# Linear layers of a hybrid encoder step: one matmul on unsplit 32-bit operands instead of three on rounded parts, weights in a ring of four pairs

## The chip, the cores and the metric

The kernel runs on one core of a Trainium2 chip. The metric is the device time of one execution in microseconds (us), as the median of several runs. The engines are named as in the profile: PE is TensorE's matmul side and PEld its weight load, DVE is VectorE, ACT ScalarE, POOL GpSimd, SP SyncE (here only an issuer of DMAs).

## The reference, cut to what matters

One inference step of two layers is computed for 512 prompt tokens and 32 sample tokens, which the kernel keeps side by side as 544 columns. Every sub-layer is a norm, a shift and scale from a condition vector, the sub-layer itself, a second norm, a gate and a residual addition. All inputs are float32.

```python
def swiglu(h, w_gate, w_up, w_down):
    return (jax.nn.silu(h @ w_gate) * (h @ w_up)) @ w_down

def forward(x, c, w, past):
    for l in range(DEPTH):                      # DEPTH = 2, D_MODEL = 1024, D_FF = 4096
        mod = (jax.nn.silu(c) @ w['ada_w'][l] + w['ada_b'][l]).reshape(B, 3, 3, D_MODEL)
        x = ffn_sublayer(x, w, mod, l, 0, 0)
        h = modulate(x, w['norm_pre'][l, 1], mod[:, 1, 0], mod[:, 1, 1])
        y, st = mixer_ab(...) if l % 2 == 0 else mixer_gdn(...)
        x = add_branch(x, y, w['norm_post'][l, 1], mod[:, 1, 2], 1.0)
        x = ffn_sublayer(x, w, mod, l, 2, 1)
```

The attention mixer (ab) has one input projection (`h @ ab_w_in`), two groups of eight heads and one output projection; the recurrent mixer (gdn) has one input projection, a short convolution, a chunked triangular solve with a scan over chunks, and one output projection. The linear layers are thus four feed-forwards of three matrices each and four projections.

## The kernel before, in words

**Units and pairs.** All weights of the linear layers are laid out in DRAM in the order of use, as 232 pairs of 1 MB (`w_stream`). A pair is two units; a unit makes one tile of 128 output features for all 544 tokens. Its weights are eight blocks of 128x128 (k = 0 to 7 over 1024 inputs), and the tokens are two halves of 272 columns (b), which go to two PSUM banks. Unit 0 of a pair uses banks 0 and 1, unit 1 banks 2 and 3. Each of the four feed-forwards has four blocks (kb) of 12 pairs: eight pairs of a gate tile and an up tile, then four pairs of the down projection. The attention input has 15 pairs, the recurrence's input 17, the two output projections 4 each.

**Three matmuls for one product.** Weights and activations are split into a high part, rounded to the type float32r, and a low part, the rest. A product of a block is `w_hi*hi + w_hi*lo + w_lo*hi`, three matmuls into the same bank (line 578; in a stage's first pair, line 600). So a unit has 48 matmuls and a pair 96.

**Who makes the parts.** GpSimd makes the weights' parts, per unit `w_hi` (line 491) and `w_lo` (line 494), from `raw`, two slots of one pair. There is one `w_hi` and one `w_lo` per unit of a pair, so GpSimd waits for `unit_done` of the pair before, and TensorE waits for `w_split` ahead of each unit. SP loads the next pair into a slot of `raw` once both units in it are split (line 477). VectorE and ScalarE make the activations' parts: after a norm, VectorE scales a row (line 1576), ScalarE applies shift and scale once or twice (line 1115), VectorE casts every other row (line 1581) and subtracts (line 1583). Within a feed-forward VectorE multiplies gate and up (line 1603), casts (line 1606) and subtracts (line 1608). Attention's outputs and the recurrence's gated outputs are cast and subtracted too.

**The order around it.** All engines run instruction lists written out by hand, with loops where a list repeats. `first_pair` is a stage's first pair: TensorE waits for one activation row k after the other (`h_ready`), and unit 1 follows unit 0 by four rows. In the first three feed-forwards VectorE also sums products for later modulation vectors, two instructions per gate and up pair (line 1532), and TensorE turns the sums with matmuls of one column, a quarter of them between the two units of each down pair (line 562, `ada_total`). Line 616 and line 609 sum squares over the features with a matrix of ones, in plain float32. In the attention's input stage TensorE computes score dots between units; in the recurrence's input stage it sums squared lengths between pairs (line 855), and near the end sums those of the sample (line 862). Between a stage's last matmul and the next stage's first come sums of squares (line 1593 on VectorE), a reciprocal root, the addition to x (VectorE six rows of eight, GpSimd two: `add_branch`) and a new norm. GpSimd splits the next stage's first pair before its additions.

The lines that the change touches most are `split_unit` and `split_pair` on GpSimd, `unit` and `first_pair` on TensorE, `modulate` on ScalarE, and `normalise` and `ffn` on VectorE.

Of the kernel before, what the change touches and what calls it, by code (L numbers as in the profile page):

```python
# [15 lines left out]
F32 = mybir.dt.float32  # L16
F32R = mybir.dt.float32r
# [4 lines left out]
P = 128  # L22
D = 1024
# [23 lines left out]
OUT_PAIRS = KD // 2  # L47
PAIRS = 4 * FFN_PAIRS + AB_PAIRS + GDN_PAIRS + 2 * OUT_PAIRS

# [13 lines left out]
def first_pairs():  # L63

    at, out = 0, {}
    for name, n in (("ffn0", FFN_PAIRS), ("ab_in", AB_PAIRS), ("ab_out", OUT_PAIRS), ("ffn1", FFN_PAIRS),
                    ("ffn2", FFN_PAIRS), ("gdn_in", GDN_PAIRS), ("gdn_out", OUT_PAIRS), ("ffn3", FFN_PAIRS)):
        out[name] = at
        at += n
    assert at == PAIRS and PAIRS % 2 == 0  # L70
    return out
# [46 lines left out]
def build(nc, io):  # L118
    with ExitStack() as ctx:
# [9 lines left out]
        hid_hi = sb("hid_hi", [P, KD, T], F32R)  # L129
        hid_lo = sb("hid_lo", [P, KD, T], F32R)  # L130
        h_at = nc.sbuf_base
        h_hi = sb("h_hi", [P, KD, T], F32R)
        h_lo = sb("h_lo", [P, KD, T], F32R)
        raw = sb("raw", [P, 2, 2, D])
        w_hi = sb("w_hi", [P, 2, D], F32R)
        w_lo = sb("w_lo", [P, 2, D], F32R)
# [31 lines left out]
        h32 = cut("k t", k=2, t=T)  # L168
# [76 lines left out]
        g_sq, g_out = cut("r t", r=2, t=T), cut("r t", r=2, t=T)  # L245
# [14 lines left out]
        w_loaded = [sem("w_loaded0"), sem("w_loaded1")]  # L260
        w_rounded = sem("w_rounded")
        w_split = sem("w_split")
# [21 lines left out]
        h32_ready = sem("h32_ready")  # L284
        h_rounded = sem("h_rounded")
        h_ready = sem("h_ready")
        hid_rounded = sem("hid_rounded")
        hid_ready = sem("hid_ready")
# [28 lines left out]
        o_rounded = sem("o_rounded")  # L317
# [59 lines left out]
        g_own = sem("g_own")  # L377
# [81 lines left out]
        def _(sp):  # L459
# [11 lines left out]
            for s in range(2):  # L471
                sp.dma_start(raw[:, s], io["w_stream"][s]).then_inc(w_loaded[s], 16)
            with sp.Fori(1, PAIRS // 2) as i:
                for s in range(2):
# [12 lines left out]
        def _(pool):  # L487
            pool.wait_ge(consts, 1)
# [8 lines left out]
            def split_pair(i, s):  # L497

                for u in range(2):
                    pool.wait_ge(w_loaded[s], 16 * i + 16)  # L500

                    pool.wait_ge(unit_done, 4 * i + 2 * s + u - 1)
                    split_unit(s, u, 4 * i + 2 * s + u)

            def split_pairs(a, b):
                if a % 2:
                    split_pair(a // 2, 1)
                with pool.Fori(a // 2 + a % 2, b // 2) as i:
                    for s in range(2):
                        split_pair(i, s)  # L510
                if b % 2:
                    split_pair(b // 2, 0)

# [9 lines left out]
            pool.wait_ge(w_loaded[0], 16)  # L523
            for u in range(2):
                split_unit(0, u, u)

            done = 1
            ends = [FIRST[name] + 1 for name in ("ab_in", "ffn1", "ffn2", "gdn_in", "ffn3")] + [PAIRS]
# [7 lines left out]
        def _(pe):  # L536
# [30 lines left out]
            def unit(u, n, hi, lo, ready=None, tail_ready=None):  # L567

                pe.wait_ge(w_split, 2 * n + u + 1)
                pe.wait_ge(bank_free[u], n + 1)  # L570
                for k in range(KD):
                    if ready:
                        ready(k)
                    for b in range(2):
                        w = slice(k * P, (k + 1) * P)
                        t = slice(b * HT, (b + 1) * HT)
                        for i, (a, m) in enumerate(((w_hi, hi), (w_hi, lo), (w_lo, hi))):
                            mm = pe.matmul(psum[:, 2 * u + b, 0:HT], a[:, u, w], m[:, k, t],  # L578
                                           start=(k == 0 and i == 0), stop=(k == KD - 1 and i == 2))
                mm.then_inc(unit_done, 1)  # L580

            def first_pair(n, hi, lo, ready):


                for u in range(2):
                    pe.wait_ge(bank_free[u], n + 1)
                pe.wait_ge(w_split, 2 * n + 2)
                lag = KD // 2
                for step in range(KD + lag):
                    for u in range(2):  # L590
# [5 lines left out]
                        for b in range(2):  # L596
                            w = slice(k * P, (k + 1) * P)
                            t = slice(b * HT, (b + 1) * HT)
                            for i, (a, m) in enumerate(((w_hi, hi), (w_hi, lo), (w_lo, hi))):
                                mm = pe.matmul(psum[:, 2 * u + b, 0:HT], a[:, u, w], m[:, k, t],  # L600
# [1615 lines left out]
```

## Time and profile before

The median of three runs is 3967.1 us (3966.59 to 3969.22). The profiled execution's own span is 3966.7 us; the page gives no time around it.

| engine | busy us | share of the span | instructions |
|---|---|---|---|
| PE | 3697.3 | 93% | 26506 |
| PEld | 3441.6 | 87% | 26506 |
| DVE | 1991.0 | 50% | 2200 |
| ACT | 580.2 | 15% | 1157 |
| POOL | 2197.0 | 55% | 956 |

Matmuls are pipelined, and one's duration covers its whole way through the array; a matmul's rate is therefore read from the starts of a series, not from the duration of one. The granted clock of TensorE is 1.00 (2.4 GHz) in most slices of the span; it falls to 0.53 in one slice of the recurrence. 343 MB move by DMA, 86 GB/s over the span. The stages in order of time: modulation head to about 70 us, first feed-forward to 724, attention input to 976, attention to 1228, its output projection to 1280, second feed-forward to 1959, third to 2593, recurrence's input to 2866, solve and recurrence to 3271, its output projection to 3321, fourth feed-forward to 3939, last addition and store to the end.

### The profile page before, as it was taken

To read this page: it belongs to the slowest core of one execution; us is meant where nothing else is said; L and a number is where in the kernel's file an instruction comes from. 1 tells how busy PE (TensorE), PEld (TensorE's weight loads), DVE (VectorE), ACT (ScalarE), POOL (GpSimd) and SP (SyncE) were. 2 spreads that over 40 slices of the span, in tenths; PEclk is the share of its full clock that TensorE was granted. 3 is DMA by queue.
4 is the path that set the end of the run, shared out by engine and by line. 5 is a ranking of instruction groups with operands and counts; after the bars stand their busy time and mean duration, and the time that the engine had idled before them with its cause. 6 is when DMAs were issued, how large, how long until landed. Compare 5 with 4: busy or idle time off the path is not lost.

```text
span 3966.7 us, 63424 instructions
## 1 busy us (share of the span) xinstructions
PE 3697.3 (93%) x26506; PEld 3441.6 (87%) x26506; DVE 1991.0 (50%) x2200; ACT 580.2 (15%) x1157; POOL 2197.0 (55%) x956
## 2 busy tenths in 40 slices
PE   6999999899999899999899999989889997999997
PEld 3999999778567899999789999978878777999997
DVE  5734636549533737356553443566765335322334
ACT  2000000321332200000210000042132123000001
POOL 3767767556003567667666777756600005777775
PEclk9999999899789999999899999989999658999998
DMA  5333323243001324223122232212300001222221
GB/s 204 136 108 111 136 101 118 78 107 131 7 22 43 106 97 144 106 106 140 64 95 101 105 113 100 101 56 75 79 9 1 1 1 54 85 87 93 85 85 65
DMA packets 80752, 342.75 MB, mean 86 GB/s; under 512 B 13960, under 2 KB 17544, under 8 KB 50936
## 3 DMA queue, kind: packets, MB, share of 16 engines
q1 hardware_dynamic: 36976, 248.02, 17.6%
q10 hardware_dynamic: 43656, 93.04, 7.3%
q8 instruction: 86, 1.41, 0.1%
q14 instruction: 34, 0.28, 0.0%
HBM read 329.93 MB, written 11.11 MB: 86 GB/s over the span
## 4 chain that ended last, share of the span: by engine, by line
PE 74%; issue 12%; POOL 6%; DVE 5%; ACT 2%; ACTq 1%; POOLq 0%; DVEq 0%
PE psum L578 61%; POOL w_lo L494 3%; POOL w_hi L491 2%; PE psum L562 2%; DVE arena L1532 1%; PE psum L1001 1%; PE psum L983 1%; PE psum L943 1%; PE psum L955 1%; PE psum L1004 1%; PE psum L1002 1%; PE psum L958 1%; ACTq L1141 1%; PE psum L545 1%; PE psum L616 1%
## 5 line engine op out<-in xcount | busy, mean ns | idle before, releaser
L491 POOL TENSOR_TENSOR w_hi<-raw,one_col 128x1024 fp32r<-128x1024 f32 x464 | 934.7, 2014 | 1682.9 <-PE psum L600 829.4
L578 PE MATMUL psum<-h_hi,w_hi 128*128 128x272 f32 x5120 | 1489.5, 291 | 21.9 <-POOL w_lo L494 16.1
L578 PE MATMUL psum<-h_hi,w_lo 128*128 128x272 f32 x5120 | 1481.5, 289 | 0.0
L578 PE MATMUL psum<-h_lo,w_hi 128*128 128x272 f32 x5120 | 1477.8, 289 | 0.0
L494 POOL TENSOR_TENSOR w_lo<-raw,w_hi 128x1024 fp32r<-128x1024 f32 x464 | 1221.2, 2632 | 36.4
L578 PEld LDWEIGHTS psum<-h_hi,w_hi 128*128 128x128 f32 x5120 | 965.2, 189 | 43.1 <-issue 42.0
L578 PEld LDWEIGHTS psum<-h_lo,w_hi 128*128 128x128 f32 x5120 | 965.4, 189 | 0.2 <-issue 0.2
L578 PEld LDWEIGHTS psum<-h_hi,w_lo 128*128 128x128 f32 x5120 | 964.5, 188 | 0.0
L578 PE MATMUL psum<-hid_hi,w_hi 128*128 128x272 f32 x2048 | 607.4, 297 | 0.6
L578 PE MATMUL psum<-hid_hi,w_lo 128*128 128x272 f32 x2048 | 600.1, 293 | 0.0
L578 PE MATMUL psum<-hid_lo,w_hi 128*128 128x272 f32 x2048 | 598.0, 292 | 0.0
L1603 DVE TENSOR_TENSOR arena<-arena,psum 128x544 f32<-128x544 f32 x128 | 92.3, 721 | 655.8 <-PE psum L578 635.9
L1615 DVE TENSOR_TENSOR arena<-arena,psum 128x544 f32<-128x544 f32 x128 | 92.1, 720 | 643.9 <-PE psum L578 643.9
L578 PEld LDWEIGHTS psum<-hid_hi,w_hi 128*128 128x128 f32 x2048 | 394.5, 193 | 3.4 <-issue 1.9
L578 PEld LDWEIGHTS psum<-hid_lo,w_hi 128*128 128x128 f32 x2048 | 394.5, 193 | 0.0
L578 PEld LDWEIGHTS psum<-hid_hi,w_lo 128*128 128x128 f32 x2048 | 393.4, 192 | 0.0
L1135 ACT ACTIVATE arena<-psum 128x544 f32<-128x544 f32 x128 | 80.0, 625 | 2096.2 <-PE psum L578 2092.0
L1532 DVE SCALAR_TENSOR_TENSOR arena<-arena,c_t 128x1536 f32<-128x1536 f32 (+1 forms) x182 | 368.3, 2064 | 0.0
L1608 DVE TENSOR_TENSOR hid_lo<-arena,hid_hi 128x544 fp32r<-128x544 f32 x128 | 358.4, 2800 | 4.4
L1606 DVE CAST hid_hi<-arena 128x544 fp32r<-128x544 f32 x128 | 193.3, 1510 | 4.4
L600 PE MATMUL psum<-h_hi,w_hi 128*128 128x272 f32 x256 | 84.1, 329 | 40.7 <-DVE h_lo L1583 39.2
L562 PEld LDWEIGHTS psum<-ones,arena 128*128 128x128 f32 x528 | 72.3, 214 | 38.5 <-DVE arena L1532 37.6
(284 smaller groups left out, 3328.3 us busy)
## 6 DMA issues: line engine op xcount, KB each, us to landing
raw<-in_w_stream SPq DMA_DIRECT2D x232, 1024.0 KB, 4.8
arena<-in_ada_w ACTq DMA_DIRECT2D x72, 768.0 KB, 5.6
arena<-in_ada_w ACTq DMA_DIRECT2D x32, 384.0 KB, 4.3
spare<-in_ada_w ACTq DMA_DIRECT2D x5, 768.0 KB, 16.9
rel_spread<-arena ACTq DMA_DIRECT2D x1, 3072.0 KB
spare_h<-in_ada_w ACTq DMA_DIRECT2D x3, 768.0 KB, 15.7
x<-in_x_t SPq DMA_DIRECT2D x1, 2176.0 KB, 18.6
out_y_t<-x SPq DMA_DIRECT2D x1, 2176.0 KB, 7.0
```

What stands on the lines that cost most here:

```text
L491: pool.tensor_tensor(w_hi[:, u], raw[:, s, u], one_col[:].broadcast_to([P, D]), ALU.mult)\
L494: pool.tensor_tensor(w_lo[:, u], raw[:, s, u], w_hi[:, u].bitcast(F32), ALU.subtract)\
L545: mm = pe.matmul(psum[0:2, b, :], c_t[:, k, :], ada_second[k][:, b * 512:(b + 1) * 512], start=(k == 0), stop=(k == KD - 1))
L562: mm = pe.matmul(psum[:, 7, 2 * t + g:2 * t + g + 1], ada_sum[:, g, t * P:(t + 1) * P], ones[:, 0:1], start=True, stop=True)
L578: mm = pe.matmul(psum[:, 2 * u + b, 0:HT], a[:, u, w], m[:, k, t], start=(k == 0 and i == 0), stop=(k == KD - 1 and i == 2))
L600: mm = pe.matmul(psum[:, 2 * u + b, 0:HT], a[:, u, w], m[:, k, t], start=(k == 0 and i == 0), stop=(k == KD - 1 and i == 2))
L1135: act.activation(split(silu[:, j % 2]), halves(0), ACT.Silu).then_inc(bank_free[0], 1)
L1532: op = dve.scalar_tensor_tensor(ada_sum[:, g, 0:n], ada_w[:, k, 0:n], c_t[:, k, g:g + 1], ada_sum[:, g, 0:n], ALU.mult, ALU.add)
L1603: dve.tensor_tensor(split(h32[:, j % 2]), split(silu[:, j % 2]), halves(2), ALU.mult)\
L1606: dve.tensor_copy(hid_hi[:, j], h32[:, j % 2]).then_inc(hid_rounded, 1)
L1608: dve.tensor_tensor(hid_lo[:, j], h32[:, j % 2], hid_hi[:, j].bitcast(F32), ALU.subtract)\
L1615: dve.tensor_tensor(split(y[:, m]), split(y[:, m]), halves(2 * (m % 2)), ALU.add)\
```

## The change

The type float32r, the parts and everything that makes them go. `w_ring` holds four pairs of unsplit weights, and the activations are one float32 tile each, `h_in` after a norm and `hid` within a feed-forward (the room that the parts had stays allocated, since other stages reuse it). A product is one matmul instruction in the program, on two float32 operands. SP loads a slot of the ring as soon as `unit_done` says that TensorE has done both units of the pair that was in it; TensorE waits for a pair's load itself, once per pair (`pair_loaded`). GpSimd keeps only its share of `add_branch`. On ScalarE a row takes one pass after a norm, whose end is `h_ready`; on VectorE the casts and subtractions go, and a down projection's rows are ready when `bank_free[1]` counts the multiplication of gate and up. Because a wait for a load has to name a slot, TensorE's lists are written out over a block of 12 pairs (first block apart, then a loop over three), where they were loops over single pairs.

```diff
-            with sp.Fori(1, PAIRS // 2) as i:
-                for s in range(2):
-                    sp.wait_ge(w_split, 4 * i - 2 + 2 * s)
-                    sp.dma_start(raw[:, s], io["w_stream"][2 * i + s]).then_inc(w_loaded[s], 16)
+            with sp.Fori(1, PAIRS // SLOTS) as i:
+                for s in range(SLOTS):
+                    sp.wait_ge(unit_done, 2 * (SLOTS * (i - 1) + s + 1))
+                    sp.dma_start(w_ring[:, s], io["w_stream"][SLOTS * i + s]).then_inc(w_loaded[s], 16)
...
-            def split_unit(s, u, n):
-                pool.tensor_tensor(w_hi[:, u], raw[:, s, u], one_col[:].broadcast_to([P, D]), ALU.mult)\
-                    .then_inc(w_rounded, 1)
-                pool.wait_ge(w_rounded, n + 1)
-                pool.tensor_tensor(w_lo[:, u], raw[:, s, u], w_hi[:, u].bitcast(F32), ALU.subtract)\
-                    .then_inc(w_split, 1)
...
-            for n, end in enumerate(ends):
-                split_pairs(done, end)
-                done = end
+            for n in range(LAYERS * SUBS):
                 add_branch(n)
...
-            def unit(u, n, hi, lo, ready=None, tail_ready=None):
-                pe.wait_ge(w_split, 2 * n + u + 1)
+            def unit(u, n, slot, of, ready=None):
                 pe.wait_ge(bank_free[u], n + 1)
                 for k in range(KD):
                     if ready:
                         ready(k)
                     for b in range(2):
-                        w = slice(k * P, (k + 1) * P)
-                        t = slice(b * HT, (b + 1) * HT)
-                        for i, (a, m) in enumerate(((w_hi, hi), (w_hi, lo), (w_lo, hi))):
-                            mm = pe.matmul(psum[:, 2 * u + b, 0:HT], a[:, u, w], m[:, k, t],
-                                           start=(k == 0 and i == 0), stop=(k == KD - 1 and i == 2))
+                        mm = pe.matmul(psum[:, 2 * u + b, 0:HT], w_ring[:, slot, u, k * P:(k + 1) * P],
+                                       of[:, k, b * HT:(b + 1) * HT], start=(k == 0), stop=(k == KD - 1))
                 mm.then_inc(unit_done, 1)
+            def pair_loaded(at, rounds=0):
+                pe.wait_ge(w_loaded[at % SLOTS], 16 * (at // SLOTS + 1 + rounds))
...
-                    for to in (h32[:, k % 2], h_hi[:, k])[:2 - k % 2]:
-                        for g, (a, b) in enumerate(GROUPS):
-                            op = act.activation(to[:, a:b], tmp[:, k % 2, a:b], ACT.Identity,
...
-                    op.then_inc(h32_ready, 1)
+                    for g, (a, b) in enumerate(GROUPS):
+                        op = act.activation(h_in[:, k, a:b], tmp[:, k % 2, a:b], ACT.Identity,
...
+                    op.then_inc(h_ready, 1)
...
-                        dve.tensor_tensor(split(h32[:, j % 2]), split(silu[:, j % 2]), halves(2), ALU.mult)\
+                        dve.tensor_tensor(split(hid[:, j]), split(silu[:, j % 2]), halves(2), ALU.mult)\
                             .then_inc(bank_free[1], 1)
-                        dve.wait_ge(bank_free[1], n + 2)
-                        dve.tensor_copy(hid_hi[:, j], h32[:, j % 2]).then_inc(hid_rounded, 1)
-                        dve.wait_ge(hid_rounded, q + j + 1)
-                        dve.tensor_tensor(hid_lo[:, j], h32[:, j % 2], hid_hi[:, j].bitcast(F32), ALU.subtract)\
-                            .then_inc(hid_ready, 1)
```

## Rows read from the trace of the kernel before

**Rows 1.** The page: busy us of an engine, share of the span, instructions.
```profile
PE 3697.3 (93%) x26506; PEld 3441.6 (87%) x26506; DVE 1991.0 (50%) x2200; ACT 580.2 (15%) x1157; POOL 2197.0 (55%) x956
```

**Rows 2.** The page: the chain that ended last, by line, shares of the span.
```profile
PE psum L578 61%; POOL w_lo L494 3%; POOL w_hi L491 2%; PE psum L562 2%; DVE arena L1532 1%; PE psum L1001 1%; PE psum L983 1%; PE psum L943 1%; PE psum L955 1%; PE psum L1004 1%; PE psum L1002 1%; PE psum L958 1%; ACTq L1141 1%; PE psum L545 1%; PE psum L616 1%
```

**Rows 3.** The chain in order of time (start, us, what, count): last feed-forward.
```profile
3369.28 570.06 PE psum L578 x4512
```

**Rows 4.** Single lines: count, duration in ns as min/median/max, first and last start.
```profile
L616 PE MATMUL psum<-arena,ones x192: 392/393/822, 42.0 to 3345.8; 128*128 128x272 f32 x192
...
L904 PE MATMUL psum<-arena x136: 275/275/554, 2884.6 to 3086.4; 128*128 128x128 f32 x136
...
L545 PE MATMUL psum<-spare,c_t x30: 591/592/1057, 28.9 to 53.2; 128*2 128x512 f32 x30
```

**Rows 5.** TensorE in order of time: start, us from first start to last end, count.
```profile
2934.95 1.06 PE L904 MATMUL psum<-arena 128*128 128x128 f32 x8
...
53.65 7.89 PE L545 MATMUL psum<-spare_h,c_t 128*2 128x512 f32 x18
```

**Rows 6.** Windows, one per stage: length, busy us (count) of each engine, PEclk, DMA.
```profile
91.30:723.70 632.40, 610.67 (x4704) 604.73 (x4704) 344.81 (x200) 32.79 (x53) 455.24 (x189) 0.98 0.32 116
...
771.10:976.10 205.00, 197.89 (x1450) 181.50 (x1449) 121.15 (x210) 38.16 (x70) 124.57 (x57) 0.98 0.38 103
...
2006.90:2592.90 586.00, 581.85 (x4608) 580.17 (x4608) 249.85 (x200) 32.82 (x53) 427.73 (x189) 1.00 0.29 105
...
2640.80:2853.00 212.20, 203.31 (x1497) 192.97 (x1497) 156.20 (x140) 51.30 (x105) 142.00 (x61) 0.98 0.22 75
...
3368.40:3939.30 570.90, 570.06 (x4513) 569.21 (x4512) 192.51 (x133) 32.78 (x53) 403.33 (x187) 1.00 0.23 83
```

**Rows 7.** The same window view, for line 562 alone: PE and PEld busy us (count).
```profile
2006.90:2592.90 586.00, 12.02 (x96) 12.16 (x96) 1.00 0.29 105
```

**Rows 8.** TensorE in order of time, with the idle us before and its releaser.
```profile
189.89 1.44 PE L562 MATMUL psum<-ones,arena 128*128 128x1 f32 x6 [4.08 <-DVE arena L1532]
```

**Rows 9.** VectorE in order of time: the end of a gate and up block.
```profile
171.96 5.18 DVE L1532 SCALAR_TENSOR_TENSOR arena<-arena,c_t 128x1536 f32<-128x1536 f32 x2
...
173.69 3.45 DVE L1532 SCALAR_TENSOR_TENSOR arena<-arena,c_t 128x1536 f32<-128x1536 f32 x1
...
179.68 0.72 DVE L1603 TENSOR_TENSOR arena<-arena,psum 128x544 f32<-128x544 f32 x1 [2.55 <-PE psum L578]
```

**Rows 10.** The chain of waits: end of the recurrence's input.
```profile
2780.79 1.72 PE psum L855 x4
...
2835.07 5.64 PE psum L862 x32
...
2854.21 0.41 ACT arena L1369
...
2884.61 2.05 PE psum L904 x8
```

**Rows 11.** The chain of waits: the norm before the last feed-forward.
```profile
3347.74 0.74 DVE arena L1576
...
3352.06 1.12 ACT arena L1115 x2
```

**Rows 12.** TensorE in order of time: the last feed-forward's first matmul.
```profile
3351.53 0.57 PE L600 MATMUL psum<-h_hi,w_hi 128*128 128x272 f32 x1 [5.32 <-DVE h_lo L1583]
```

**Rows 13.** Windows around that first pair: the seventh column is the granted clock.
```profile
3354.00:3356.00 2.00, 1.92 (x11) 1.59 (x9) 1.75 (x4) 1.58 (x4) 0.00 (x0) 0.64 0.00 0
```

**Rows 14.** Line 1593: count, duration in ns as min/median/max.
```profile
L1593 DVE TENSOR_TENSOR arena<-arena x42: 718/1944/2645, 690.1 to 3942.1; 128x544 f32<-128x544 f32 x42
```

**Rows 15.** Waits of SP's queue: us in total, times, longest us.
```profile
SPq L477 <- POOL w_lo L494: 3720.4, 230, 417.4
```

**Rows 16.** DMA issues: count, KB each, median us to landing.
```profile
raw<-in_w_stream SPq DMA_DIRECT2D x232, 1024.0 KB, 4.8
```

**Rows 17.** Waits of the weight load: us in total, times, longest us.
```profile
PEld psum L578 <- issue: 44.1, 72, 1.7
```

More of the change, by code:

```diff
@@ L259, in build @@
         out_stored = sem("out_stored")
-        w_loaded = [sem("w_loaded0"), sem("w_loaded1")]
-        w_rounded = sem("w_rounded")
-        w_split = sem("w_split")
+        w_loaded = [sem(f"w_loaded{s}") for s in range(SLOTS)]
         unit_done = sem("unit_done")
@@ L596, in first_pair @@
                         for b in range(2):
[L597 to L600, printed above, removed]
-                                               start=(k == 0 and i == 0), stop=(k == KD - 1 and i == 2))
+                            mm = pe.matmul(psum[:, 2 * u + b, 0:HT], w_ring[:, n % SLOTS, u, k * P:(k + 1) * P],
+                                           of[:, k, b * HT:(b + 1) * HT], start=(k == 0), stop=(k == KD - 1))
                         if k == KD - 1:
@@ L644, in ffn, with pair @@
-                first_pair(n0, h_hi, h_lo, lambda k: pe.wait_ge(h_ready, KD * n_pre + k + 1))
-                with pe.Fori(1, KD) as j:
-                    gate_up(n0 + j)
-                downs(0, n0)
+                per = FFN_PAIRS // KB
+                def pair(at, kb, of, ready=None, between=None):
+                    slot = at % SLOTS
+                    pair_loaded(at, per // SLOTS * kb)
+                    unit(0, at + per * kb, slot, of, ready)
+                    if between:
+                        between()
+                    unit(1, at + per * kb, slot, of)
@@ new lines, in downs, with total @@
+                def downs(kb):
+                    def ready(k):
+                        pe.wait_ge(bank_free[1], n0 + per * kb + k + 2)
+                    for j in range(KD // 2):
+                        total = None
+                        if ADA_PARTS[f]:
+                            def total():
+                                ada_total(ADA_CHUNKS_BEFORE[f] + kb, ADA_PARTS[f], j)
+                        pair(n0 + KD + j, kb, hid, None if j else ready, total)
+                first_pair(n0, h_in, lambda k: pe.wait_ge(h_ready, KD * n_pre + k + 1))
@@ L648, in ffn @@
+                for j in range(1, KD):
+                    pair(n0 + j, 0, h_in)
+                downs(0)
                 with pe.Fori(1, KB) as kb:
-                    first = n0 + kb * (FFN_PAIRS // KB)
-                    with pe.Fori(0, KD) as j:
-                        gate_up(first + j)
-                    downs(kb, first)
+                    for j in range(KD):
+                        pair(n0 + j, kb, h_in)
+                    downs(kb)
             pe.wait_ge(c_ready, 1)
@@ L662, in _, with pair_of, product @@
             norm_sum(2)
-            def product(first, pairs, hi, lo, ready=None):
+            def pair_of(n, of):
+                pair_loaded(n)
+                for u in range(2):
+                    unit(u, n, n % SLOTS, of)
+            def product(first, pairs, ready=None):
                 if ready:
-                    first_pair(first, hi, lo, ready)
-                with pe.Fori(first + bool(ready), first + pairs) as n:
-                    unit(0, n, hi, lo)
-                    unit(1, n, hi, lo)
+                    first_pair(first, h_in, ready)
+                for n in range(first + bool(ready), first + pairs):
+                    pair_of(n, h_in)
             def rel_bias():
@@ L1733, in outputs @@
             def outputs(e):
-                mixer, i, h = items[e]
+                mixer, i, head = items[e]
                 k0 = 4 * (mixer == "B")
```

134 lines of the change are left out of this document (36 added, 98 removed).

## The prediction

> **What bounds the kernel now.** I read the page's busy times first: TensorE has work in flight for 93% of the span [rows 1]. The chain of work that ended last comes next: 61% of the span is line 578 alone, the matmuls of the linear layers, and the two splitting lines of GpSimd (491 and 494) follow with 5% together [rows 2]. So TensorE's rate is the bound, and GpSimd enters only where TensorE waits for a split. The chain of the last feed-forward stage has no such wait: 4512 matmuls in 570.06 us without a break, 126.3 ns from one start to the next [rows 3]. Three of them make one product of a 128x128 weight block with 272 tokens: 379 ns. A pair of units has 32 such products: 12.13 us, and there are 232 pairs.
>
> **The price of one unsplit product.** The trace already holds plain 32-bit matmuls. Each that the kernel issues stands as two instructions: the six row sums of line 616 issue 96, and the trace has 192 [rows 4]. What one costs from start to start at 272 columns I take from both sides. Eight of 128 columns with a new stationary block each run in 1.06 us, less the last one's 0.275, over 7: 112 ns; eighteen of 512 columns in 7.89 us, less 0.592, over 17: 429 ns [rows 4, 5]. The durations are 275, 393 and 592 ns for 128, 272 and 512 columns [rows 4], so 272 columns are 118 above the first and 199 below the second: 112 + 118 = 230 and 429 - 199 = 230. I take 230 ns, with 228 and 234 as ends (the durations leave the rate of a long dense stream open). One product is then 2 x 230 = 460 ns against 379 for the three of today: two slow instructions cost more than three quick ones. A pair takes 64 x 0.230 = 14.72 us, 2.59 more than now; over 232 pairs that is +601.
>
> **What comes off, stage by stage** (stretches begin behind a stage's first pair) [rows 6].
> - Last feed-forward: 47 pairs x 14.72 = 691.8 for 570.9: +120.9.
> - Third: the same 47 pairs and the 96 small modulation matmuls of line 562, 12.0 us [rows 7], are 703.8 for 586.0: +117.8.
> - First and second: twice the small matmuls, 24, make 715.8 for 632.4: +83.4 each (the second has the same pattern). They take 632.4 - 598.0 = 34.4 more than the third with twice its small matmuls, and that is what the splits cost there today. Four times in each, TensorE stands 4.08 us before line 562 [rows 8], because VectorE has still to finish line 1532, behind the rounding and subtracting of the hidden tile. One of the two instructions of line 1532 takes 5.18 - 3.45 = 1.73 us and the other 3.45 while GpSimd reads beside it [rows 9]. Afterwards VectorE has 0.72 + 2 x 1.73 = 4.2 us behind the last gate and up pair, and TensorE fills 7.36 us with the first unit of the down projection before it asks: this wait goes, and nothing is late next. Were VectorE still to take 3.45 twice, 0.72 + 6.9 would be 0.3 over. If all of the 34.4 stayed in both stages, it is +69.
> - Attention's input: 14 pairs; the 35.2 us that today are not matmuls of line 578 (205.0 - 14 x 12.13: score dots and their waits for ScalarE) stay: +36.3.
> - Recurrence's input: 15 pairs 220.8, the row sums 8 x 1.72 and 5.6 [rows 10] are 240.2 for 212.2: +28.0. The stalls that vanish are VectorE's convolutions, which run beside GpSimd today. The sixteenth pair costs nothing: from ScalarE's line 1369 at 2854.21, which needs the fifteenth, a chain of 30.4 us leads to TensorE's next work at 2884.61 [rows 10], and 14.72 lies inside it.
> - The two output projections: 8 x 2.59 = +20.7.
> - First pairs, six after a normalisation: today VectorE's scaled row at 3347.74 leads, over two passes of ScalarE and a subtraction, to the first matmul at 3351.53 [rows 11, 12]. With one pass of 1.12 behind the 0.74 it is due at 3349.6: -1.9 each, -11.4. ScalarE then delivers a row in about 1.1 us and TensorE needs 0.92 or, at the clock granted there until about 3355 (half, 1.2 GHz) [rows 13], 1.84: it is TensorE that paces, and the pair takes some 14.7 and 2 for the clock, about the 16.9 of today. No gain there.
> - Stage ends: the last sum of squares (line 1593), for which TensorE waits, takes up to 2.65 beside GpSimd's split of the next stage's first pair, and 0.72 with GpSimd still [rows 14]: -1.9 at five ends, -9.5.
> - Attention itself, the solve and the recurrence hold no split; the outputs of attention lose one VectorE pass, worth 0 to -10; I take 0.
>
> Sum: 120.9 + 117.8 + 166.8 + 36.3 + 28.0 + 20.7 - 11.4 - 9.5 = +470 on the profiled execution's 3966.7, which is 0.4 below the median of the runs: 4436.
>
> **The ring and the queues.** SP's queue stood 3720 us for GpSimd's splits [rows 15]; now it stands for units of TensorE, four pairs back. A pair's megabyte lands in a median of 4.8 us [rows 16], and three pairs, 44 us, lie between a slot's release and its next use: TensorE's new wait for a load, once per pair, ends at once. Queued behind it is all that follows on TensorE, its pair first. By the same figures two slots would do: the ring gains nothing. At the start four megabytes are issued instead of two behind the same load; TensorE asks for the first only behind the head's modulation products. GpSimd loses 928 instructions and keeps its additions to x, now without splits queued ahead.
> TensorE's loops become longer and fewer: a turn holds twelve pairs. Waits put down to issue ahead of line 578's weight loads were 44.1 us in 72 times, 1.7 at most [rows 17], nearly all with matmuls still running. Twelve turns of 1.7 are 20, the upper bound; I take 0.
> The Trainium skill (Runtime: NRT & Kernel Launch, Instruction fetch mechanics) says that a taken branch to code outside the pages at hand stalls for a fetch; this trace has only short loops, and no row here shows what a long one costs.
>
> **Rivals.**
> 1. Each pass keeps the price of a pass in the dense stream. 272 columns in 126.3 ns are slower than the plain matmuls per column and pass (115 of 230), so the dense stream may carry something, 11 ns a pass, that short bursts do not show. Then a product is 4 x 126.3 = 505 ns, 45 above mine: 7424 x 0.0454 = +337, 4773. For it: the bursts of rows 5 last a microsecond or eight. Against it: line 855's four instructions of 512 columns, directly behind the dense matmuls, take 1.72 us, 430 each [rows 10], as slow as without that stream. By the Trainium skill (FP8 and Floating Point Precision, TensorE Precision Notes) a true 32-bit product is four passes through the array; counted in today's passes that is this rival, and the two instructions of double length here agree with the four. 7%.
> 2. Not slower: the two instructions of a product overlap, because they use the same weight block and tokens. It decides where an instruction's pace falls from 230 to 230 - 470/14.848 = 198 ns; if only one of the two counted, it would be 7424 x 0.230 less, near 2730. Against it: the pairs of rows 5 do not overlap. 3%.
> 3. A new wait takes the split's place: the turns of the longer loops, or late weights. A microsecond at each pair would be +232, 4668. For it: code and ring are new. Against it: rows 16 and 17. 5% beyond my range.
> 4. The ring frees nothing: that is my forecast already, and changes no number.
>
> **How the numbers follow.** My case has 85%. Its own range: 228 ns is -30 and attention -10, which makes 4396; 234 is +59, the splits' cost in the first two feed-forwards +69: 4505 at most of one alone. The range 4395 to 4520 leaves out the two slow rivals and the fast one, 15%. A measurement here tells 0.2%, 8 us, from no change. Faster 0.03, same 0.01, slower 0.96.
>
> **What would show it.** In the profile after: line by line, two instructions of 128x272 per product, 14848 in all, 229 to 232 ns from start to start in the last feed-forward's chain, some 692 us; no 4 us gap ahead of line 562's matmuls; SP waiting for TensorE; VectorE's last sum of squares at 0.72 at every stage end. A pace of 253 is rival 1; gaps once in twelve pairs are rival 3. I am wrong if the last feed-forward's stretch is below 660 or above 720.

## The result: slower by 11.3%, and the profile after

The kernel after takes 4413.8 us (median of four runs, 4406.4 to 4419.8) against 3967.4 (3966.6 to 3969.2): ratio 1.1126, interval 1.1110 to 1.1141. The forecast was 4436, 22 us above it. The profiled execution has a span of 4412.8, 446.1 more than before.

The page after: busy times [rows 1], then the chain that ended last by engine and by line [rows 2].

```profile
PE 4231.3 (96%) x19082; PEld 3414.2 (77%) x19082; DVE 1111.7 (25%) x1822; ACT 553.6 (13%) x1109; POOL 42.4 (1%) x28
...
PE 66%; DVE 2%; ACT 1%; issue 0%; ACTq 0%; DVEq 0%
PE psum L530 54%; PE psum L553 2%; PE psum L959 1%; PE psum L941 1%; PE psum L901 1%; PE psum L913 1%; PE psum L962 1%; PE psum L569 1%; PE psum L960 1%; PE psum L916 1%; PE psum L518 1%; DVE x L1583 0%; PE psum L862 0%; DVE arena L1581 0%; PE psum L928 0%
```

GpSimd is gone from the chain, which could be followed back to 1318.6 us only (its shares add up to 70% of the span, so they are not to be set beside those of rows 2). VectorE has lost 879 us of work, and TensorE has 7424 instructions fewer and yet more to do. The chain in order of time, as in rows 3 (line 530 is the old 578, line 518 the old 562, line 553 the first pair):

```profile
1544.46 1.23 PE psum L518 x12
1545.70 14.78 PE psum L530 x64
...
3696.05 689.35 PE psum L530 x3008
```

The last line gives the pace: 689.35 / 3008 = 229.2 ns from start to start, two of them 458 ns where three took 379. The small modulation matmuls follow the unit ahead of them without a gap; the 4.08 us of rows 8 are no longer there. The stages as windows, in the order and with the columns of rows 6:

```profile
90.03:800.80 710.77, 710.77 (x3200) 592.57 (x3199) 153.51 (x136) 32.73 (x53) 0.00 (x0) 1.00 0.32 103
844.43:1082.97 238.54, 232.39 (x1001) 179.60 (x1000) 94.59 (x222) 38.15 (x69) 0.00 (x0) 0.99 0.33 87
2189.13:2889.18 700.05, 700.05 (x3105) 581.90 (x3103) 105.50 (x136) 32.75 (x53) 0.00 (x0) 1.00 0.27 88
2933.11:3176.00 242.89, 238.62 (x1024) 191.13 (x1024) 79.44 (x140) 50.86 (x105) 0.00 (x0) 1.00 0.19 65
3696.05:4385.39 689.34, 689.34 (x3009) 571.17 (x3007) 48.98 (x69) 32.73 (x53) 0.00 (x0) 1.00 0.20 67
```

In the three feed-forward windows TensorE's busy time is the whole length: no gap is left, neither at a turn of the longer loops nor at a load. (The windows of the recurrence's input end at different work before and after; the table below goes to the stage's last matmul in both.)

Where the 446 us came from, by the first and last matmuls of each stage in the two traces (us, after less before; "ahead" is from the last matmul of the stage before to the first of this one, "rest" from behind the first pair to the last matmul):

```
stage               ahead   first pair   rest                forecast of the rest
first feed-forward   -1.9      +0.7      +78.3               +83.4
attention input      -4.4      +0.6      +33.6               +36.3
attention output     -7.0   3.6 + 6.6 = 10.2, whole stage    +10.4 (ahead: 0)
second feed-forward  -4.2      +1.1      +79.1               +83.4
third feed-forward   -4.6      +0.8     +114.0              +117.8
recurrence input     -4.9      +0.9      +32.4               +28.0
recurrence output    -0.1   2.4 + 6.6 = 9.0, whole stage     +10.4
last feed-forward    -4.3      -1.7     +118.4              +120.9
```

The rounded entries sum to +446. As a balance: 232 pairs at 14.67 instead of 12.13 us are +589, and 143 come back: 81 in the first two feed-forwards, 31 ahead of the stages, 13 in the first pairs, 17 in the rest (each rounded).

### The profile page after: what moved, and what is told of

It is laid out like the page before. It is cut to its first block, busy times and chain, and to the rows that moved or that the text cites. A ratio compares the mean times of both kernels' runs of the same rounds, so it can differ in the third digit from the quotient of the medians.

```text
span 4412.8 us, 44833 instructions
## 1 busy us (share of the span) xinstructions
PE 4231.3 (96%) x19082; PEld 3414.2 (77%) x19082; DVE 1111.7 (25%) x1822; ACT 553.6 (13%) x1109; POOL 42.4 (1%) x28
## 4 chain that ended last, share of the span: by engine, by line
PE 66%; DVE 2%; ACT 1%; issue 0%; ACTq 0%; DVEq 0%
PE psum L530 54%; PE psum L553 2%; PE psum L959 1%; PE psum L941 1%; PE psum L901 1%; PE psum L913 1%; PE psum L962 1%; PE psum L569 1%; PE psum L960 1%; PE psum L916 1%; PE psum L518 1%; DVE x L1583 0%; PE psum L862 0%; DVE arena L1581 0%; PE psum L928 0%
## 5 line engine op out<-in xcount | busy, mean ns | idle before, releaser
L530 PE MATMUL psum<-h_in,w_ring 128*128 128x272 f32 x10240 | 2356.6, 393 | 4.3 <-ACT spare L1308 4.3
L530 PEld LDWEIGHTS psum<-h_in,w_ring 128*128 128x128 f32 x10240 | 1945.1, 190 | 415.1 <-issue 14.9
L530 PE MATMUL psum<-hid,w_ring 128*128 128x272 f32 x4096 | 953.1, 393 | 0.0
L530 PEld LDWEIGHTS psum<-hid,w_ring 128*128 128x128 f32 x4096 | 774.6, 190 | 156.7
L1547 DVE TENSOR_TENSOR hid<-arena,psum 128x544 f32<-128x544 f32 x128 | 92.3, 721 | 1545.6 <-PE psum L530 1499.4
L1554 DVE TENSOR_TENSOR arena<-arena,psum 128x544 f32<-128x544 f32 x128 | 92.3, 721 | 849.6 <-PE psum L530 849.6
L1486 DVE SCALAR_TENSOR_TENSOR arena<-arena,c_t 128x1536 f32<-128x1536 f32 (+1 forms) x182 | 276.9, 1566 | 0.0
L553 PE MATMUL psum<-h_in,w_ring 128*128 128x272 f32 x512 | 136.0, 432 | 21.2 <-ACT h_in L1069 20.7
L553 PEld LDWEIGHTS psum<-h_in,w_ring 128*128 128x128 f32 x512 | 107.5, 212 | 48.9 <-issue 23.3
L569 PE MATMUL psum<-arena,ones 128*128 128x272 f32 x192 | 66.0, 509 | 31.4 <-ACT arena L1026 31.4
L518 PE MATMUL psum<-ones,arena 128*128 128x1 f32 x528 | 63.8, 246 | 0.0
L688 PE MATMUL psum<-arena 64*128 64x128 f32 (+3 forms) x128 | 59.4, 550 | 0.0
L901 PEld LDWEIGHTS psum<-spare_h 128*128 128x128 f32 x336 | 42.5, 196 | 14.7 <-DVE spare_h L1892 11.4
## 6 DMA issues: line engine op xcount, KB each, us to landing
x<-in_x_t SPq DMA_DIRECT2D x1, 2176.0 KB, 18.4
```

Source lines behind the costliest of these rows:

```text
L518: mm = pe.matmul(psum[:, 7, 2 * t + g:2 * t + g + 1], ada_sum[:, g, t * P:(t + 1) * P], ones[:, 0:1], start=True, stop=True)
L530: mm = pe.matmul(psum[:, 2 * u + b, 0:HT], w_ring[:, slot, u, k * P:(k + 1) * P], of[:, k, b * HT:(b + 1) * HT], start=(k == 0), stop=(k = ...
L553: mm = pe.matmul(psum[:, 2 * u + b, 0:HT], w_ring[:, n % SLOTS, u, k * P:(k + 1) * P], of[:, k, b * HT:(b + 1) * HT], start=(k == 0), stop ...
L569: mm = pe.matmul(psum[:, 4 + b, 0:HT], ones[:], sq[:, k % 2, b * HT:(b + 1) * HT], start=(k == 0), stop=(k == KD - 1))
L688: pe.matmul(psum[:, b, 0:n], z[r:r + HD, zq + c, i * P:(i + 1) * P], z[r:r + HD, zk + c, 0:n], start=True, stop=False, skip_group_check=(m ...
L901: mm = pe.matmul(psum[:, b + 3, t], low_m[:, u, t], inv_t[:, u, t], start=True, stop=True)
```

## Experiments

Ratios are to the kernel before on the same chip (3967.0 us for the first four, 3968.5 for the others).

**1. The ring with two slots.** The kernel after with one number changed:

```diff
-SLOTS = 4
+SLOTS = 2
```

> The changed kernel with a ring of two pairs instead of four. My theory: the ring adds nothing, because a pair's megabyte lands in 4.8 us and one pair of TensorE takes 14.67, so even with one pair between release and next use no load is late: 4414 us, within 8, and no gap of TensorE behind a wait for a load. Rival (the four slots hide loads that run into the 768 KB modulation loads): some of the 232 pairs wait a few us, 4450 or more, with TensorE's idle time put down to DMAs in the three feed-forwards that load modulation weights.

Measured: 4413.6 us (4409.6 to 4415.8), ratio 1.1125 [1.1107, 1.1144], and the stages as with four (the profiled executions differ in two stretches that hold no wait for a load: 4.6 us less in the recurrence, 2.7 more in the last first pair). The first feed-forward's window and SP's wait:

```profile
90.00:800.80 710.80, 710.75 (x3200) 593.19 (x3199) 153.56 (x137) 32.72 (x53) 0.00 (x0) 1.00 0.31 103
```

```profile
SPq L467 <- PE psum L530: 3205.2, 222, 21.4
```

710.80 with two slots, 710.77 with four. With four, SP's wait and the loads are these:

```profile
SPq L467 <- PE psum L530: 3193.3, 220, 21.4
```

```profile
w_ring<-in_w_stream SPq DMA_DIRECT2D x232, 1024.0 KB, 4.8
```

A load lands in 4.8 us where even two slots leave it a pair's 14.7. Two slots more are neither cost nor gain; what follows is about the arithmetic and about the work that went with the parts.

**2. GpSimd as busy as before, with nobody waiting for it.** The kernel of experiment 1; GpSimd rounds and subtracts on tiles of its own at the times of the old splits, and no matmul reads the results. It is added work only; the outputs come from the same arithmetic as in experiment 1.

```diff
+            def split_unit(n):
+                pool.tensor_tensor(w_hi[:], src[:], one_col[:].broadcast_to([P, D]), ALU.mult).then_inc(w_rounded, 1)
+                pool.wait_ge(w_rounded, n + 1)
+                pool.tensor_tensor(w_lo[:], src[:], w_hi[:].bitcast(F32), ALU.subtract).then_inc(w_split, 1)
...
+                split_pairs(done, end)
+                done = end
                 add_branch(n)
```

> The changed kernel with two slots, in which GpSimd again does the arithmetic of the old split, at its old places, but from a tile of its own into tiles that nobody reads; nobody waits for it except its own additions to x. It shows what the old kernel paid for GpSimd reading beside VectorE, without the casts, the subtractions and the waits for splits. My theory: only the stage ends come back (1.9 at five ends) and at most 0.3 at each of eight modulation sums, since 0.72 + 2 x 3.45 = 7.6 us on VectorE stand against 7.36 of TensorE: 4420 to 4435. Rival: the contention itself was what the first two feed-forwards paid, and their 34 us each come back: 4480.

Measured: 4432.5 us (4429.7 to 4438.1), ratio 1.1176 [1.1158, 1.1195]: 19 more than experiment 1. The time ahead of five stages grows by 2.3 to 3.1 us each, and ahead of attention's output by nothing (245.7 us, as in the kernel after). The rest of the 19 is made of smaller parts: 3.8 in the first two feed-forwards, 1.9 in attention's input, 4.4 in the recurrence (where experiment 1 had 4.6 less than the kernel after) and -4.7 in the first pairs. Line 1574 here is the last sum of squares of rows 14; first this kernel, then the kernel after (count, ns as min/median/max, first and last start):

```profile
L1574 DVE TENSOR_TENSOR arena<-arena x42: 718/1943/2645, 762.6 to 4406.1; 128x544 f32<-128x544 f32 x42
```

```profile
L1538 DVE TENSOR_TENSOR arena<-arena x42: 715/717/726, 760.8 to 4388.2; 128x544 f32<-128x544 f32 x42
```

With GpSimd busy it has the 718/1944/2645 of rows 14 to within a nanosecond, with GpSimd idle never more than 726. So the gain at the stage ends is GpSimd's silence, as the prediction said, at 2.3 to 3.1 us instead of 1.9; and what attention gained (-7.0) is not. The first two feed-forwards each pay 2 us and no more: the slow VectorE lines are back, but the rounding and subtracting ahead of them are not, and VectorE is done about when TensorE ends the first unit of the down projection, as the prediction reckoned.

GpSimd's own instruction, same kernel (busy us, mean ns):

```profile
L497 POOL TENSOR_TENSOR w_lo<-src,w_hi 128x1024 fp32r<-128x1024 f32 x464 | 1207.0, 2601 | 36.5
```

The longest addition to VectorE's 0.72 is 1.93 us, less than one such instruction of 2.6. What it depends on stands at the end of the stage before the last feed-forward, VectorE's two sums first, then GpSimd's two instructions:

```profile
3667.86 1.94 DVE L1574 TENSOR_TENSOR arena<-arena 128x544 f32<-128x544 f32 x1
...
3669.94 2.65 DVE L1574 TENSOR_TENSOR arena<-arena 128x544 f32<-128x544 f32 x1
```

```profile
3667.32 1.89 POOL L495 TENSOR_TENSOR w_hi<-src,one_col 128x1024 fp32r<-128x1024 f32 x1 [2.72 <-PE psum L566]
...
3669.30 2.71 POOL L497 TENSOR_TENSOR w_lo<-src,w_hi 128x1024 fp32r<-128x1024 f32 x1
```

Each sum ends just behind the GpSimd instruction that ran when it began: 3669.80 behind 3669.21, 3672.59 behind 3672.01, 0.59 and 0.58 us. So do 39 of the 42 of line 1574 in this trace and 39 of the 42 of line 1593 in the kernel before, each 0.58 to 0.59 us behind; the other three of each begin with GpSimd idle and take 0.72. A sum waits for the rest of the GpSimd instruction and only then runs. The Trainium skill (SBUF — State Buffer, Who interferes with whom) has it that a VectorE instruction with two inputs in SBUF contends with a GpSimd instruction that reads SBUF, and that the ports they share are an exclusive lock; the trace agrees, by these ends.

**3. The kernel before, with the small matmuls moved behind the second unit.** The split arithmetic stays.

```diff
                             unit(0, first + KD + j, hid_hi, hid_lo, None if j else ready)
-                            ada_total(ADA_CHUNKS_BEFORE[f] + kb, ADA_PARTS[f], j)
                             unit(1, first + KD + j, hid_hi, hid_lo)
+                            ada_total(ADA_CHUNKS_BEFORE[f] + kb, ADA_PARTS[f], j)
```

> The kernel before with one change: a quarter of the modulation sums (line 562) goes behind the second unit of a down pair instead of between its two units. My theory: TensorE then asks about 6 us later than today, VectorE is done, and the eight waits of 4.1 us and the slow clock behind each (about 2.2 us) go: some 50 us, 3917. Rival 1: the wait is only moved, since VectorE's next work or the rounding is late by as much: 3960 or more. Rival 2: the waits go but the clock loss has another cause: about 33 us, 3934.

Measured: 3903.7 us (3902.4 to 3910.7), ratio 0.9846 [0.9830, 0.9863]: 63 less than before. The first feed-forward's window (632.40 in rows 6):

```profile
91.30:692.10 600.80, 595.31 (x4695) 590.45 (x4695) 344.88 (x200) 32.81 (x53) 455.22 (x189) 1.00 0.34 122
```

The first two stages lose 31.4 and 30.5 of the 34.4 that the prediction had put down to the splits, the third 5.1. So 31 of those 34.4 go by the order of two lines, with all splits kept. They were the price of the splits' work on VectorE in that order only; the changed kernel removes them by taking the work away, and the kernel before can have them for nothing. VectorE's and GpSimd's busy times are those of rows 6, so it is the place of the wait and not the work that went. Half of the gain is the wait itself (TensorE is idle for 5.5 us of the window instead of 21.7), the other half is the clock behind it: busy time falls from 610.67 to 595.31 us, at a mean granted clock of 0.98 and 1.00. Behind the wait of rows 8 the trace has 0.50 (1.2 GHz) until some 197 us.

**4. The kernel before, with 16-bit parts.** Both rounded parts are bfloat16, still three matmuls; the parts carry fewer digits, so this computes less exactly than before.

```diff
-F32R = mybir.dt.float32r
+F32R = mybir.dt.bfloat16
...
```

> The kernel before with all high and low parts in bfloat16 instead of float32r: still three matmuls for a product, less exact. It asks why a pass of the old kernel takes 126 ns where 272 columns at 2.4 GHz are 113 and a plain 32-bit half takes 229 = 227 + 2. Theory A (the four-byte operands of the quick form cost about 10 ns a matmul): the pace falls to 116 ns, 22272 x 0.010 = 220 us off, 3745, less what GpSimd then bounds, since its 5.8 us a unit stand against 5.6 of TensorE in the first two feed-forwards. Theory B (a matmul with a new weight block each time cannot go quicker, whatever its type): 126 ns stays, and the time is within 30 us of 3967, lower only by quicker casts.

Measured: 3764.9 us (3762.9 to 3766.7), ratio 0.9489 [0.9473, 0.9505]. From its chain, a dense stretch of the last feed-forward:

```profile
3564.85 128.76 PE psum L580 x1110
```

128.76 / 1110 = 116.0 ns for the same 272 columns that took 126.3 [rows 3]. The page's lines of the high parts, matmuls and weight loads:

```profile
L580 PE MATMUL psum<-h_hi,w_hi 128*128 128x272 bf16 x5120 | 1431.5, 280 | 41.6 <-POOL w_lo L496 30.7
L580 PEld LDWEIGHTS psum<-h_hi,w_hi 128*128 128x128 bf16 x5120 | 501.4, 98 | 157.8 <-issue 65.1
```

A weight load is recorded at 98 ns here, at 189 for the parts of the kernel before and 190 for the 32-bit words of the kernel after. The 10 ns a pass therefore belonged to the four-byte quick form and not to dense streams. Whether the weight load or the moving operand carries it stays open: operands of mixed width were not tried.

**5. The kernel after, with the squared lengths one by one.** In the recurrence's input one row of squared lengths (line 814) stands behind each unit instead of two behind each pair.

```diff
-                    pair_of(n0 + p, h_in)
-
-                    for m in (2 * p - 6, 2 * p - 5):
+                    pair_loaded(n0 + p)
+                    for u in range(2):
+                        unit(u, n0 + p, (n0 + p) % SLOTS, h_in)
+                        m = 2 * p - 6 + u
                         if 0 <= m < 2 * NH:
```

> The changed kernel with one edit in the recurrence's input: the two squared lengths that stood behind a pair stand one behind each unit. It asks for the 0.61 us that TensorE still waits ahead of seven pairs there, which the prediction had taken for VectorE beside GpSimd. My theory now: a ring of waits (TensorE's lengths release ScalarE's squares, behind which stands ScalarE's copy of the next unit, behind which TensorE waits for the bank); with one length at a time the copy is done while the unit runs: the seven gaps fall below 0.3, some 4 us less, 4408 to 4412. Rival: ScalarE's copies follow VectorE's convolutions, and the gaps stay at 0.6 in their sum.

What it is to explain, from the kernel after: the chain between two pairs, and TensorE's next matmul with the idle time before it.

```profile
2994.34 0.87 PE psum L814 x2
...
2995.30 0.04 ACT arena L1318
...
2995.83 0.28 ACT arena L1307
...
2996.34 0.20 ACT spare L1308
...
2996.67 14.91 PE psum L530 x64
```

```profile
2996.67 0.70 PE L530 MATMUL psum<-h_in,w_ring 128*128 128x272 f32 x2 [0.61 <-ACT spare L1308]
```

Seven times TensorE stands 0.61 us for ScalarE's copies (lines 1307 and 1308), which free the accumulators, and ScalarE stands for TensorE's second squared length through its squares (1318). One run, not repeated: 4401.6 us, and TensorE between the same units:

```profile
2975.24 1.02 PE L814 MATMUL psum<-arena 128*128 128x512 f32 x2
2976.10 7.49 PE L530 MATMUL psum<-h_in,w_ring 128*128 128x272 f32 x32
2983.43 1.02 PE L814 MATMUL psum<-arena 128*128 128x512 f32 x2
2984.29 7.49 PE L530 MATMUL psum<-h_in,w_ring 128*128 128x272 f32 x32
```

Each group starts before the modelled end of the one ahead and none has an idle time; the seven gaps are gone, and the stage's rest is 6.0 us shorter. The gaps are 7 x 0.61 = 4.3 of it, and what TensorE loses in starting again is the rest: a pair with its two lengths takes 17.23 us in the kernel after and 2 x 8.19 = 16.38 here. The profiled execution is another 7 us shorter, and these are not the edit's: 4.4 lie ahead of the recurrence's output, where experiment 1, without this edit, has 4.6 less too, and the rest mostly in first pairs, which follow the clock (see below).

**6. Experiments 3 and 4 together.**

```diff
-F32R = mybir.dt.float32r
+F32R = mybir.dt.bfloat16
...
-                            ada_total(ADA_CHUNKS_BEFORE[f] + kb, ADA_PARTS[f], j)
                             unit(1, first + KD + j, hid_hi, hid_lo)
+                            ada_total(ADA_CHUNKS_BEFORE[f] + kb, ADA_PARTS[f], j)
```

> The kernel before with both edits: bfloat16 parts and the modulation sums behind the second unit. If the two gains are of different origin they add: 3765 - 63 = 3702. If with the quicker passes TensorE asks again before VectorE is done (a unit is now 5.6 us instead of 6.05), part of the waits stays: 3715 to 3735.

Measured: 3694.0 us (3691.5 to 3696.2), ratio 0.9310 [0.9294, 0.9325]; the sum of the two gains would have been 3702 (5.8 of the difference lie in attention, 259.9 us for the 265.7 of experiment 4). The window of the first feed-forward and what TensorE waits for:

```profile
91.19:652.03 560.84, 545.73 (x4696) 458.73 (x4695) 346.49 (x200) 32.74 (x53) 434.28 (x189) 1.00 0.36 131
```

```profile
PE psum L580 <- POOL w_lo L496: 35.4, 56, 1.0
```

The kernel before has this for the same wait:

```profile
PE psum L578 <- POOL w_lo L494: 16.1, 32, 0.9
```

560.84 - 545.73 = 15 us of this stage are idle. With quicker passes GpSimd's splits show more: 35.4 us over the whole kernel for 16.1.

**7. The same, with the hidden tile's rounding on ScalarE.**

```diff
                         act.activation(split(silu[:, j % 2]), halves(0), ACT.Silu).then_inc(bank_free[0], 1)
+                        act.wait_ge(bank_free[1], n + 2)
+                        act.activation(hid_hi[:, j], h32[:, j % 2], ACT.Copy).then_inc(hid_rounded, 1)
...
-                        dve.tensor_copy(hid_hi[:, j], h32[:, j % 2]).then_inc(hid_rounded, 1)
```

> As the kernel with bfloat16 parts and later sums, and ScalarE rounds the hidden tile's high part instead of VectorE. Theory: VectorE loses 1.5 us a gate and up pair, so it reads less beside GpSimd, GpSimd's splits end earlier, and the gaps of about 0.5 us ahead of TensorE's gate and up pairs in the first two feed-forwards shrink: some 20 us less, 3680. Rival: those gaps come from line 1532 alone, and nothing moves: 3702, or ScalarE's rounding delays its gate activations and it is slower.

Measured: 3677.8 us (3676.5 to 3678.8), ratio 0.9268 [0.9252, 0.9283], the fastest of all and ahead of both kernels. The same two views:

```profile
90.75:643.91 553.16, 545.73 (x4695) 458.73 (x4695) 301.96 (x168) 53.76 (x85) 434.82 (x189) 1.00 0.39 133
```

```profile
PE psum L580 <- POOL w_lo L496: 19.6, 44, 1.0
```

VectorE's 44 us of rounding went to ScalarE, which takes 21 us for it and had room, and the idle time of the stage halves from 15.1 to 7.4.

**8. The same, with GpSimd splitting the next stage's first pair behind its additions to x.**

```diff
-            ends = [FIRST[name] + 1 for name in ("ab_in", "ffn1", "ffn2", "gdn_in", "ffn3")] + [PAIRS]
+            ends = [FIRST[name] for name in ("ab_in", "ffn1", "ffn2", "gdn_in", "ffn3")] + [PAIRS]
```

> As the one with ScalarE's rounding, and GpSimd splits a stage's first pair behind its additions to x instead of ahead of them. Theory: the last sum of squares of a stage is then at 0.72 instead of up to 2.65, which is worth 1.9 at each of five stage ends: 9 us less than the kernel without this edit. Rival: the splits then run beside VectorE's additions to x, which are on the way to the next norm, and take back as much or more.

Measured: 3697.5 us (3696.6 to 3706.0), ratio 0.9324 [0.9308, 0.9339]: 20 slower than experiment 7. The chain at the stage end before the last feed-forward, first here, then in experiment 7:

```profile
3095.55 0.74 DVE arena L1597
...
3107.83 2.30 DVE x L1647
3110.13 2.58 DVE arena L1645
```

```profile
3079.59 2.43 DVE arena L1597
...
3086.47 1.73 DVE x L1647
3088.20 1.78 DVE arena L1645
```

The sum of squares is quick, as wanted, and the additions to x behind it pay instead, several of them. The contention moved to a place where it costs more; the first matmul behind each of the five stage ends is 3.3 to 5.2 us later than in experiment 7.

## Why the prediction was right, and where it missed

**The price held.** 230 ns a half product was taken from bursts of 128 and 512 columns [rows 4, 5]; 3008 in a row give 229.2. At 14848 instructions 0.8 ns is 12 us of the 22.

**Rival 1 (505 ns a product) fell** with that pace; 253 would have been its sign. Experiment 4 shows why: the 126 ns of the old passes held 10 ns that bfloat16 passes don't have, so they were no measure of what a plain pass costs. Its four passes stand, at a lower price: two recorded instructions of 229.2 are four times 114.6, near the 116.0 of a bfloat16 pass. The Trainium skill (FP8 and Floating Point Precision, TensorE Precision Notes) counts four passes for a true 32-bit product; in time the trace agrees. **Rival 2** would have needed two halves to overlap: they do not. **Rival 3** (loops, late weights) has no row to stand on, since the feed-forward windows are full. **Rival 4** was the forecast already, and experiment 1 shows it.

**The stalls of the first two feed-forwards went whole**, as taken: 78.3 and 79.1 for 83.4. The 4 to 5 us between are the price (2.4) and the 192 small matmuls of a stage: 710.8 less the 689.4 that 47 pairs take is 21.4 for the 24 taken from rows 7. Experiment 3 shows the reading of rows 8 and 9 right and its label too wide: the 34.4 were called "what the splits cost there today", and 31 of them left a kernel that still splits.

**Starts and ends of stages:** -20.9 forecast, -24.3 ahead of six stages and +2.4 in their first pairs. In the first feed-forward GpSimd's splits are over 11 us ahead of the first matmul, and it shows the start alone: -1.9, the figure of the sum. At the other five -4.2 to -4.9 less 1.9 leaves 2.3 to 3.0 for the end; experiment 2 puts 2.3 to 3.1 back. The term of 1.9 there took VectorE's line alone and left out the clock behind it. The four row sums of TensorE that follow are these windows, ahead of the recurrence's input in the kernel after and in experiment 2:

```profile
2892.70:2893.90 1.20, 1.17 (x4) 0.68 (x4) 0.00 (x0) 0.87 (x3) 0.00 (x0) 0.97 0.67 280
```

```profile
2905.10:2907.30 2.20, 2.17 (x4) 1.17 (x4) 0.00 (x0) 0.00 (x0) 0.00 (x0) 0.50 0.00 0
```

Behind the longer wait (5.46 us of idle time for 3.54) they run at the lower level and take 1.0 us more. At the last feed-forward, TensorE's first matmul now waits for ScalarE alone, 3.80 us for the 5.32 of rows 12:

```profile
3680.84 1.42 PE L553 MATMUL psum<-h_in,w_ring 128*128 128x272 f32 x5 [3.80 <-ACT h_in L1069]
```

The first pairs follow the granted clock. Windows of the second feed-forward's first pair, then of the last one's (seventh column, as in rows 13):

```profile
1416.00:1418.00 2.00, 1.50 (x4) 1.18 (x5) 1.33 (x2) 2.00 (x6) 0.00 (x0) 0.50 0.00 0
1422.00:1424.00 2.00, 2.00 (x9) 1.57 (x8) 0.17 (x1) 1.98 (x5) 0.00 (x0) 0.83 0.33 32
...
3680.00:3682.00 2.00, 1.16 (x5) 0.92 (x6) 1.17 (x3) 2.00 (x5) 0.00 (x0) 1.00 0.00 0
```

The pair that begins at the lower level (0.50, 1.2 GHz) and reaches the full one after some 6 us takes 18.0 us, the one at the full level from its start 15.2. Both stand behind the same normalisation, and what gave the last one the full clock in this execution stays open: in experiment 1 it begins at 0.50 and takes 17.95. The -1.7 of the table is luck to that extent.

**The step that failed: the recurrence's input,** 28.0 forecast and 32.4 measured. The term let all stalls there vanish, as VectorE's convolutions beside GpSimd. Seven of them were never that: the kernel before has the same seven, ended by the same line of ScalarE (1354, which is 1308 after). In all, times, longest:

```profile
PE psum L578 <- ACT spare L1354: 4.3, 7, 0.6
```

VectorE has half its work there now (79 us for 156) and they stand. They come from a ring of ScalarE and TensorE, and experiment 5 opens it by moving one squared length, which is worth 6.0 us. The other 4.6 us of idle time did vanish (8.9 in the window of rows 6, 4.3 in that of the kernel after), but with GpSimd as busy as before (experiment 2) the stage is as short as without it, 257.9 us: so its silence is not the reason there either, and the reason stays open. A slow engine beside a wait had been taken for its cause.

The 4.4 are not the seven stalls alone. From behind the first pair to the chain's line 904 (862 after) it is 243.8 us before and 274.3 after, +30.5, or 2.5 over the forecast: 6.0 for the stalls, less 0.8 for the price, 2.0 for the sample sums of rows 10 (3.66 us for 5.64) and 0.7 in the chain behind. The sixteenth pair costs nothing, as taken. The remaining 1.9 lie in the recurrence, which differs by more between kernels whose edit doesn't touch it: from the last matmul of its input to the first of its output it takes 404.6 us here and 400.0 in experiment 1.

**Attention,** taken as 0 in a range of 0 to -10, gave -7.0. Experiment 2 rules GpSimd's contention out; what is left of the change there is the dropped VectorE pass on its outputs. The traces show where it acts. 150 us behind the stage before, VectorE's line 1811 (1747 after) follows the last output copied, before with a subtraction between them, and TensorE's wait for it is 0.33 us longer. Before, then after:

```profile
1125.79 0.38 PE L738 MATMUL psum<-diag_mask,ident 128*128 128x128 f32 x1 [1.34 <-DVE arena L1811]
```

```profile
1233.58 0.49 PE L695 MATMUL psum<-diag_mask,ident 128*128 128x128 f32 x2 [1.01 <-DVE arena L1747]
```

The 17 us from there, before and after (TensorE's busy time and count first, its clock in the seventh column):

```profile
1125.80:1142.80 17.00, 17.00 (x49) 10.17 (x50) 5.22 (x24) 3.71 (x14) 0.00 (x0) 0.52 0.00 1
```

```profile
1233.60:1250.60 17.00, 17.00 (x87) 11.10 (x88) 7.51 (x36) 6.40 (x24) 0.00 (x0) 1.00 0.00 0
```

Behind the longer wait TensorE runs at its lower level, behind the shorter one at the full level. Around this place the same 84 matmuls take 25.8 us before and 17.8 after, which is more than the whole gain. All six kernels with the subtraction have the wait of 1.34 us here and a clock of 0.50 to 0.60 in the 17 us behind it; all four without it have 1.01 and 1.00. So the range held, but most of the gain is the clock and not the pass itself. The pass was not put back alone, and why the clock falls in the one case is not shown.

Of the 23.5 between sum and measured: stretches behind the first pairs 18.4 and projections 1.5 (price and small matmuls, and 2 us in attention's input that stay unexplained), attention 7.0, starts and ends 1.0, less 4.4 in the recurrence's input and behind it.

## What to carry to other kernels

Price a change of number format from start to start at the operand's own width, not by counting instructions: here two plain 32-bit instructions (2 x 229) lose to three reduced ones (3 x 126, or 3 x 116 in bfloat16), since TensorE is the bound. Before crediting a format with the stalls that leave with it, move the waiting instruction alone: the kernel before gains 63 us by exchanging two lines, where 143 came back here. A short wait can cost more in the clock behind it than in itself. Work taken off an idle-looking engine is worth what it slows beside it, and moving it elsewhere can cost more than leaving it.

## What the runs showed of the hardware that was not expected

- At 272 columns a pass of the reduced 32-bit form takes 126.3 ns and one of bfloat16 116.0; the recorded weight loads are 190 and 98 ns.
- A plain 32-bit instruction takes 112, 229 and 429 ns for 128, 272 and 512 columns: between 272 and 512 that is 0.83 ns a column, two cycles at 2.4 GHz, dense or not.
- One VectorE sum of 0.72 us becomes up to 2.65 beside GpSimd's subtraction, with no data in common: it ends 0.58 us behind the GpSimd instruction that ran when it began, 39 times of 39 (experiment 2).
- In attention, 17 us at about half the clock (0.50 to 0.60) followed a wait of 1.34 us in six kernels, and the full clock a wait of 1.01 us in four.
